# Differential attention: the next head's projections spread over eighteen of the twenty steps of a head's values, in place of sixteen

## The chip, the cores and the metric

The kernel runs on one core of one Trainium2 chip. The metric is the time on the device in microseconds (us) of one launch. Everything is fp32; matrix products are made of fp32r halves (a rounded `hi` and the rest `lo`), three matmuls for each product.

## What is computed

Two transformer blocks on a sequence of 1024 rows of width 1024. The first (pooling, gated linear attention, forgetting attention, a gated MLP) is not touched. The second is differential attention with 8 heads, each of two query and key parts of 64 and a value of 128, over 256 context keys and 1024 own keys:

```python
q, k, v, z = jnp.split(h @ w_in, 4, axis=-1)      # q and k of the own rows are rotated (axial rope)
s = jnp.einsum('bqhzd,bkhzd->bhzqk', q, k)
p = jax.nn.softmax(s, axis=-1)
a = p[:, :, 0] - lam * p[:, :, 1]
o = jnp.einsum('bhqk,bkhe->bqhe', a, v)
o = o * lax.rsqrt(jnp.mean(o * o, axis=-1, keepdims=True) + SUBLN_EPS) * subln_gain * (1 - lambda_init)
y = (o * jax.nn.silu(z)) @ w_out
```

An output projection, a residual and a last norm follow.

## The kernel before

`differential_attention` (L2099) runs on the five engines, each with its own program; semaphores alone order them. The engines call `heads` (L2183): scores of head 0, then for each head `values` (its attention times V) and the scores of the next head. Heads 0 to 6 run `values(h, True)`, which also projects Q and K of head h + 1; head 7 runs `values(7, False)` without that.

**Pieces and units.** The projections of a head are pieces: `TILE` (L2106) gives pieces 0 and 1 as the two halves of Q, 2 and 3 as the halves of K, 4 as K of the context, 5 and 6 as z; V has three more. Each piece takes 8 units (`contract`, L2705: k = 0 to 7), each unit three matmuls of 512 columns, or 256 for the context. Pieces 0 to 4 belong to `values`, the rest to `scores`. A piece's PSUM bank is `BANK` (L2108): banks 1, 2, 1, 2, 1.

**The spread.** `spread` (L2115) deals the 40 units of pieces 0 to 4, a context unit counting half, into `SHARING + 1` slots. The first slot is `before`, which TensorE runs ahead of the steps; the others are `chunks[n]`, run in step n. With SHARING = 16 these are the units (piece and k):

```
before: 00 01 02
chunks: 0: 03 04   1: 05 06   2: 07 10   3: 11 12   4: 13 14   5: 15 16   6: 17 20   7: 21 22 23   8: 24 25
        9: 26 27  10: 30 31  11: 32 33  12: 34 35  13: 36 37  14: 40 41 42 43  15: 44 45 46 47   16 to 19: none
end = [2, 6, 9, 13, 15]
```

`end[p]` (L2127) is the step in which piece p is finished. The lists `next_head` of ScalarE (L2391) and VectorE (L2597) place their work on piece p by it, and these engines work strictly in the order of their program.

**A step on TensorE** (`values`, L2801, 20 steps: 10 key tiles for each half g of the queries): `turn(n + 2)` (L2758) makes four 128x128 transposes of the probabilities into one of three banks; `times_v(n)` (L2774) makes three matmuls with V, and waits for `lo(n)` of VectorE; then the units of `chunks[n]`. In step 0 the product comes behind the units. Step 12 ends with `squares(h, 0)` (L2785), the sum of squares of the first half's output; steps 16 and 17 and the end of the loop have `turn_v` 0, 1 and 2 (L2737), transposes of the next head's V. `turn_v(1)` waits until the shuffle of piece 3 has read bank 2. `score(h + 1, 0, 0)` (L2745), the first work of the next stage, waits for all splits of Q and K (`qk_done`) and for two of the three splits of V (`v_done`).

**ScalarE in step n** (L2435): `hi(n + 2)` (L2411) rounds the transposed probabilities out of PSUM; then `next_head(n)`: `qk_hi` (L2324) of piece p at `end[p] + 2` and `+ 3` (the two parts z), of piece 4 at `end[3] + 3`; the rounding of the k weights at 2 and of the z weights at 8; `v_hi` (L2344) of V at 16, 18 and 19, the last behind `output` and `square` of the previous half; then `silu_z` at 3 and 5, `output` (L2354) at 10, `square` (L2359) at 11, `rstd` (L2363) at 13, each with what it waits for.

**VectorE in step n** (L2624): `lo(n + 2)` (L2583); then `next_head(n)`: `terms` (L2532: the cosine product and the shuffle) of piece p at `end[p]`, `rotated` (L2540: the add of cosine and sine terms) at `end[p] + 1`, `qk_lo` (L2545) at `+ 2` and `+ 3`, of piece 4 at `end[3] + 3`; `v_lo` (L2555) at 16, 18 and 19; and `gated` (L2588) at 14. Where several fall in one step, pieces come in order, and V last.

**GpSimd** (L2288): the rest `lo` of the k weights (`subtract_lo`, L2078), the sine terms (L2275) of pieces 0, 1 and 2, the rest of the z weights, the sine term of piece 3, then the rest of the v weights of the head after (`next_v`). **SyncE** (L2227): the second rope half once the terms of piece 0 are made, the z weights once piece 1 is done (`done(h + 1, 1)`), the first rope half after the terms of piece 2, then the store of the first half of the output.

Of the kernel before, what the change touches and what calls it, by code (L numbers as in the profile page):

```python
# [2098 lines left out]
def differential_attention(core, ph, mix_at, lead):  # L2099
# [15 lines left out]
    def spread(units, slots):  # L2115

        share, spent, out = sum(u[2] for u in units) / slots, 0.0, [[] for _ in range(slots)]
        for p, k, c in units:
            out[min(int(spent / share), slots - 1)].append((p, k))
            spent += c  # L2120
        return out


    SHARING = 16
    before, *chunks = spread([(p, k, 0.5 if FROM[p] == CONTEXT else 1.0) for p in range(5) for k in range(KT)], SHARING + 1)
    chunks += [[] for _ in range(STEPS - SHARING)]
    end = [max(n for n in range(STEPS) if (p, KT - 1) in chunks[n]) for p in range(5)]  # L2127
# [826 lines left out]
def program(nc, d):  # L2954

    with ExitStack() as ctx:
        core = Core(nc, ctx, d)
        with ExitStack() as first:
            mix_at = next_place(nc)
            mix = first.enter_context(nc.sbuf_tensor("mix", [P, KT, SEQ], F32))  # L2960
            with ExitStack() as rows:
                gate_rows = rows.enter_context(nc.sbuf_tensor("gate_rows", [P, SEQ], F32))
                mixers(core, mix, mix_at, gate_rows)
            core.clear_semaphores()
            hid_at = next_place(nc)
            hid = first.enter_context(nc.sbuf_tensor("hid", [P, FT, SEQ], F32))
            with Phase(core, "wo") as po, Phase(core, "gu") as pg, Phase(core, "down") as pd, Phase(core, "diff") as ph:
                lead = second_half(core, po, pg, pd, mix, mix_at, hid, hid_at)
                differential_attention(core, ph, mix_at, lead)
            core.clear_semaphores()  # L2970
        with ExitStack() as last:
            feat = last.enter_context(nc.sbuf_tensor("feat", [P, KT, SEQ], F32))
            block_output(core, feat)
# [97 lines left out]
```

How the kernel before makes its waits and increments, by code:

```python
    def __call__(self, ins):  # L66
        self.n += 1
        ins.then_inc(self.sem, 1)
        self.eng.wait_ge(self.sem, self.base + self.n)
# [90 lines left out]
    def load(self, sync, i, c, src):  # L160
        b = self.bufs[c]
        if self.in_place:
            self.wait_free(sync, i, c)
        elif self.raw.shape[1] == 2:
            sync.wait_ge(self.lo[b], self.nth(i, c) + 1)
        elif c:
            sync.wait_ge(self.lo[self.bufs[c - 1]], self.nth(i, c - 1) + 2)
        else:
            final = len(self.bufs) - 1
            before = self.bufs[final]
            sync.wait_ge(self.lo[before], self.nth(i, final) + 2 - self.uses[before])
        sync.dma_start(self.raw[:, self.raw_of[b], :], src).then_inc(self.loaded[b], 16)
# [1 line left out]
    def wait_free(self, eng, i, c):  # L175
        b = self.bufs[c]
        before = [x for x in range(c) if self.bufs[x] == b]
        if before:
            eng.wait_ge(self.piece_done, (i + 1) * self.pieces + self.last[before[-1]] + 1)
        else:
            final = [x for x in range(len(self.bufs)) if self.bufs[x] == b][-1]
            eng.wait_ge(self.piece_done, i * self.pieces + self.last[final] + 1)
# [1 line left out]
    def round_hi(self, act, i, c):  # L185
        b = self.bufs[c]
        act.wait_ge(self.loaded[b], self.nth(i, c) * 16 + 16)
        if not self.in_place:
            self.wait_free(act, i, c)
        act.activation(self.core.wh[:, b, :], self.raw[:, self.raw_of[b], :], ACT.Copy).then_inc(self.hi[b], 1)
```

## Time and profile before

| | us |
|---|---|
| median of 3 runs | 2386.15 |
| lowest and highest | 2385.19, 2386.16 |
| the profiled execution's own time | 2389.79 |
| its span | 2387.9 |
| TensorE busy | 2177.1 (91%) |
| VectorE, ScalarE, GpSimd busy | 1240.7, 993.4, 619.3 |

The span is the time from the first to the last instruction of the profiled execution; its own time lies 1.9 us above it. In the rows further down, times are us from the start of the span; a row of the timeline gives start, duration, engine, line, operation, what it writes and reads, and in brackets the engine's idle time before it with the instruction that ended it. The differential attention's stages of values and scores run from about 1482 to 2262.

### The profile page before, as it was taken

The page shows a single profiled execution, that of the slowest core. Times are in us where ns is not written, and L with a number is a line of the kernel's source. Part 1 is how long each engine was busy: PE and PEld are TensorE (multiplying, and loading weights), DVE is VectorE, ACT ScalarE, POOL GpSimd, SP SyncE. Part 2 cuts the span into 40 slices and gives each one's busy share as a digit, 9 for nine tenths or more (in the row PEclk, how much of TensorE's full clock was granted, in tenths as well). Part 3 has the DMA queues.
Part 4 walks back from the last instruction along what each step waited for, and adds up shares of the span by engine and source line. Part 5 has one row for each costly group of instructions (what it writes and reads, how often), then busy time and mean ns, then how long its engine had stood idle before and what let it go on. Part 6 is the DMA issues. An engine that isn't in the chain of part 4 may idle for free. (4 is left out here: it accounts for less than half of the span.)

```text
span 2387.9 us, 28748 instructions
## 1 busy us (share of the span) xinstructions
PE 2177.1 (91%) x10344; PEld 1772.4 (74%) x10344; DVE 1240.7 (52%) x1650; ACT 993.4 (42%) x1546; POOL 619.3 (26%) x387
## 2 busy tenths in 40 slices
PE   6998888888999999789999987999999999998668
PEld 5886777766888888678887866877778777786557
DVE  4645534435322212132445455877768777677553
ACT  4434434434311111121224344565656656566531
POOL 2212122254022222122344532212222222221140
PEclk9999999989999999899999988999999999999989
DMA  3100000004222221121423421111010110100052
GB/s 110 49 28 26 27 9 26 18 1 159 97 88 79 70 79 61 53 106 61 150 97 117 138 97 71 35 37 36 28 46 32 42 35 26 48 31 27 9 194 106
DMA packets 46687, 152.38 MB, mean 64 GB/s; under 512 B 6160, under 2 KB 6576, under 8 KB 46496
## 3 DMA queue, kind: packets, MB, share of 16 engines
q1 hardware_dynamic: 42768, 137.68, 16.8%
q0 software_dynamic: 3856, 13.86, 1.7%
q8 instruction: 39, 0.64, 0.1%
q14 instruction: 24, 0.20, 0.0%
HBM read 132.38 MB, written 18.88 MB: 63 GB/s over the span
## 5 line engine op out<-in xcount | busy, mean ns | idle before, releaser
L214 PE MATMUL psum<-h_hi,w_hi 128*128 128x512 f32 x704 | 276.2, 392 | 22.5 <-POOL w_lo L199 22.5
L215 PE MATMUL psum<-h_lo,w_hi 128*128 128x512 f32 x704 | 275.6, 391 | 0.0
L216 PE MATMUL psum<-h_hi,w_lo 128*128 128x512 f32 x704 | 275.4, 391 | 0.0
L2378 ACT ACTIVATE diff_probs<-psum,diff_neg_max 128x1280 f32<-128x1280 f32 x128 | 170.3, 1330 | 130.1 <-DVE diff_neg_max L2563 129.3
L2563 DVE TENSOR_REDUCE diff_neg_max<-psum 128x1 f32<-128x1280 f32 x128 | 189.5, 1487 | 56.1 <-PE psum L2035 56.0
L199 POOL TENSOR_TENSOR w_lo<-w_whole,w_hi 128x1024 fp32r<-128x1024 f32 x44 | 107.2, 2439 | 391.4 <-ACT w_hi L190 391.4
L2092 PE MATMUL psum<-h_hi,w_hi 128*128 128x512 f32 x496 | 200.8, 405 | 6.5 <-DVE h_lo L1463 3.9
L1823 DVE SCALAR_TENSOR_TENSOR gu_ada_product<-gu_ada_w,gu_cond 128x1024 f32<-128x1024 f32 x48 | 91.1, 1898 | 214.3 <-DMA gu_ada_w<-in_ada_w 211.3
L2093 PE MATMUL psum<-h_lo,w_hi 128*128 128x512 f32 x496 | 196.4, 396 | 0.0
L2094 PE MATMUL psum<-h_hi,w_lo 128*128 128x512 f32 x496 | 195.9, 395 | 0.0
L214 PEld LDWEIGHTS psum<-h_hi,w_hi 128*128 128x128 f32 x704 | 133.2, 189 | 51.5 <-issue 23.6
L1834 DVE TENSOR_TENSOR down_a_lo<-hid,down_a_hi 128x512 fp32r<-128x512 f32 x44 | 101.6, 2310 | 128.6 <-ACT down_a_hi L1743 126.4
L2034 PE MATMUL psum<-diff_k_hi_lo,diff_q_hi_twice 128*128 128x512 f32 (+1 forms) x384 | 142.5, 371 | 24.7 <-DVE diff_v_lo L2558 13.4
L2283 POOL TENSOR_SCALAR diff_probs<-diff_probs,diff_recip 128x1280 f32<-128x1280 f32 x64 | 85.9, 1342 | 291.7 <-DVE diff_probs L2580 291.7
L390 PE MATMUL psum<-h_hi,w_hi 128*128 128x512 f32 x368 | 153.6, 417 | 2.5 <-POOL w_lo L379 1.4
L216 PEld LDWEIGHTS psum<-h_hi,w_lo 128*128 128x128 f32 x704 | 133.1, 189 | 28.0
L215 PEld LDWEIGHTS psum<-h_lo,w_hi 128*128 128x128 f32 x704 | 133.3, 189 | 27.4
L391 PE MATMUL psum<-h_lo,w_hi 128*128 128x512 f32 x368 | 146.9, 399 | 0.0
L392 PE MATMUL psum<-h_hi,w_lo 128*128 128x512 f32 x368 | 146.8, 399 | 0.0
L190 ACT ACTIVATE w_hi<-w_whole 128x1024 fp32r<-128x1024 f32 x44 | 46.5, 1061 | 238.3 <-DMA w_whole<-in_w_gu 238.2
L1657 POOL TENSOR_TENSOR w_lo<-down_w_raw,w_hi 128x1024 fp32r<-128x1024 f32 x42 | 101.0, 2407 | 135.7 <-ACT w_hi L1741 135.7
L2035 PE MATMUL psum<-diff_k_hi_lo,diff_q_lo_twice 128*128 128x512 f32 (+1 forms) x384 | 132.0, 359 | 0.0
(374 smaller groups left out, 4883.7 us busy)
## 6 DMA issues: line engine op xcount, KB each, us to landing
w_whole<-in_w_gu SPq DMA_DIRECT2D x44, 512.0 KB, 3.4
down_w_raw<-in_w_down SPq DMA_DIRECT2D x44, 512.0 KB, 3.4
w_whole<-in_da_w_in SPq DMA_DIRECT2D x31, 512.0 KB, 3.5
gu_ada_w<-in_ada_w SPq DMA_DIRECT2D x24, 512.0 KB, 4.3
w_whole<-in_w_in SPq DMA_DIRECT2D x23, 512.0 KB, 3.4
diff_rope_half<-in_rope SPq DMA_DIRECT2D x17, 512.0 KB, 4.1
mix<-in_x SPq DMA_DIRECT2D x8, 512.0 KB, 8.7
wo_w_raw<-in_w_o SPq DMA_DIRECT2D x8, 512.0 KB, 3.4
```

What stands on the lines that cost most here:

```text
L214: pe.matmul(out, wh, rh, start=(k == 0), stop=False)
L215: pe.matmul(out, wh, rl, start=False, stop=False)
L216: last = pe.matmul(out, wl, rh, start=False, stop=(k == KT - 1))
L390: pe.matmul(out, wh, rh, start=(k == 0), stop=False)
L391: pe.matmul(out, wh, rl, start=False, stop=False)
L392: last = pe.matmul(out, wl, rh, start=False, stop=(k == KT - 1))
L2034: pe.matmul(out, self.q_hi[:, z, queries], self.k[:, z, keys], start=True, stop=False)
L2092: pe.matmul(out, wh, rh, start=(k == 0), stop=False)
L2093: pe.matmul(out, wh, rl, start=False, stop=False)
L2094: last = pe.matmul(out, wl, rh, start=False, stop=(k == KT - 1))
L2378: act.activation(dst, core.psum[:, 1536 * z:1536 * z + NKEY], ACT.Exp, bias=nm[:, qb % 2, z:z + 1], accum_out=rs[:, qb % 2, z:z + 1]).then ...
L2563: dve.tensor_reduce(nm[:, qb % 2, z:z + 1], core.psum[:, 1536 * z:1536 * z + NKEY], AX.X, ALU.max, negate=True).then_inc(s[f"max{z}"], 1)
```

## The change

```diff
-    SHARING = 16
+    SHARING = 18
     before, *chunks = spread([(p, k, 0.5 if FROM[p] == CONTEXT else 1.0) for p in range(5) for k in range(KT)], SHARING + 1)
     chunks += [[] for _ in range(STEPS - SHARING)]
     end = [max(n for n in range(STEPS) if (p, KT - 1) in chunks[n]) for p in range(5)]
```

The lists become:

```
before: 00 01
chunks: 0: 02 03   1: 04 05   2: 06 07   3: 10 11   4: 12 13   5: 14 15   6: 16 17   7: 20 21   8: 22   9: 23 24
       10: 25 26  11: 27 30  12: 31 32  13: 33 34  14: 35 36  15: 37 40  16: 41 42 43 44  17: 45 46 47  18, 19: none
end = [2, 6, 11, 15, 17]
```

Nothing else is changed: the same instructions are issued, in another order on TensorE, ScalarE and VectorE.

## Rows read from the trace of the kernel before

**Rows 1.** The page: busy time of TensorE, and issue to landing of a weight load.
```profile
PE 2177.1 (91%) x10344; PEld 1772.4 (74%) x10344; DVE 1240.7 (52%) x1650; ACT 993.4 (42%) x1546; POOL 619.3 (26%) x387
...
w_whole<-in_da_w_in SPq DMA_DIRECT2D x31, 512.0 KB, 3.5
```

**Rows 2.** Waits of TensorE, 1484 to 2185 us: total, times, longest.
```profile
PE psum L2780 <- DVE diff_pt_lo L2585: 14.8, 14, 1.9
PE psum L2787 <- ACT diff_rstd L2361: 6.7, 7, 1.0
```

**Rows 3.** Timeline of TensorE: the first product with V of heads 0, 1, 2.
```profile
1534.08 0.50 PE L2780 MATMUL psum<-diff_pt_hi,diff_v_hi 128*128 128x512 f32 x1 [0.56 <-DVE diff_pt_lo L2585]
...
1634.97 0.50 PE L2780 MATMUL psum<-diff_pt_hi,diff_v_hi 128*128 128x512 f32 x1 [0.21 <-DVE diff_pt_lo L2585]
...
1734.37 0.50 PE L2780 MATMUL psum<-diff_pt_hi,diff_v_hi 128*128 128x512 f32 x1 [0.20 <-DVE diff_pt_lo L2585]
```

**Rows 4.** Stretches behind heads 0 and 1: busy PE, PEld, DVE, ACT, POOL; PEclk, DMA.
```profile
1582.20:1585.60 3.40, 3.40 (x12) 2.51 (x10) 1.32 (x2) 2.42 (x4) 0.77 (x1) 0.52 0.00 0
1683.10:1686.50 3.40, 3.40 (x17) 2.50 (x16) 1.82 (x2) 2.44 (x5) 0.75 (x1) 1.00 0.00 0
```

**Rows 5.** Timeline of TensorE, head 0: step 10 and the start of step 11's product.
```profile
1558.54 0.48 PE L2780 MATMUL psum<-diff_pt_hi,diff_v_hi 128*128 128x512 f32 x1
...
1559.32 0.39 PE L2092 MATMUL psum<-h_hi,w_hi 128*128 128x512 f32 x1
...
1560.01 0.39 PE L2092 MATMUL psum<-h_hi,w_hi 128*128 128x512 f32 x1
...
1561.05 0.48 PE L2780 MATMUL psum<-diff_pt_third,diff_v_hi 128*128 128x512 f32 x1
```

**Rows 6.** Timeline of TensorE, head 0: `squares` of step 12, two context units of step 14.
```profile
1566.85 1.12 PE L2787 MATMUL psum<-diff_rstd,diff_ones 128*128 128x512 f32 x2 [0.97 <-ACT diff_rstd L2361]
1567.81 0.60 PE L2770 MATMUL psum<-ident,diff_probs 128*128 128x128 f32 x4
...
1571.46 0.28 PE L2092 MATMUL psum<-hc_hi,w_hi 128*128 128x256 f32 x1
...
1571.81 0.28 PE L2092 MATMUL psum<-hc_hi,w_hi 128*128 128x256 f32 x1
```

**Rows 7.** Timeline of TensorE, head 0: the last product and the next head's first score.
```profile
1581.31 0.50 PE L2780 MATMUL psum<-diff_pt_hi,diff_v_hi 128*128 128x512 f32 x1 [1.87 <-DVE diff_pt_lo L2585]
...
1582.24 0.72 PE L2034 MATMUL psum<-diff_k_hi_lo,diff_q_hi_twice 128*128 128x512 f32 x1
```

**Rows 8.** Timelines of VectorE and GpSimd, head 0: piece 2 (K, second half).
```profile
1560.02 0.69 DVE L2537 TENSOR_TENSOR diff_rope_cos<-psum,diff_rope_half 128x512 f32<-128x512 f32 x1
...
1562.85 2.80 DVE L2543 TENSOR_TENSOR diff_rope_cos<-diff_rope_cos,diff_rope_sin 128x512 f32<-128x512 f32 x1 [0.92 <-POOL diff_rope_sin L2277]
...
1562.70 2.40 POOL L2081 TENSOR_TENSOR w_lo<-w_whole,w_hi 128x1024 fp32r<-128x1024 f32 x1
```

**Rows 9.** Timeline of ScalarE, head 0: `rstd` begins, and `hi(16)` behind it.
```profile
1569.14 1.28 ACT L2365 ACT_TABLE_LOAD   x1
...
1572.98 0.58 ACT L2416 ACTIVATE diff_pt_hi<-psum 128x512 fp32r<-128x512 f32 x1
```

**Rows 10.** Timeline of VectorE, head 0: from `lo(16)` to `v_lo(1)`, 12 rows in all.
```profile
1573.59 0.69 DVE L2585 TENSOR_TENSOR diff_pt_lo<-psum,diff_pt_hi 128x512 fp32r<-128x512 f32 x1 [1.70 <-ACT diff_pt_hi L2416]
1574.20 0.68 DVE L2543 TENSOR_TENSOR diff_rope_cos<-diff_rope_cos,diff_rope_sin 128x512 f32<-128x512 f32 x1
1574.80 0.75 DVE L2592 SCALAR_TENSOR_TENSOR diff_rstd<-diff_o,subg,diff_rstd 128x512 f32<-128x512 f32 x1
...
1576.19 0.68 DVE L2585 TENSOR_TENSOR diff_pt_third<-psum,diff_pt_third 128x512 fp32r<-128x512 f32 x1
...
1579.06 0.88 DVE L2030 TENSOR_TENSOR diff_k_hi_lo<-psum,diff_k_hi_lo 64x256 fp32r<-64x256 f32 x2
...
1581.17 0.68 DVE L2558 TENSOR_TENSOR diff_v_lo<-psum,diff_v_hi 128x512 fp32r<-128x512 f32 x1
```

## The prediction

> **What bounds the kernel now.** The page comes first: TensorE is busy for 91% of the span [rows 1]. The change touches only `values(h, True)`, the value stage of seven of the eight heads, so I then read the waits of TensorE over those heads. Two are large: the products with V wait for VectorE's `lo` (L2585), 14.8 us in 14 waits, two in each head, and `squares` waits for ScalarE (L2361), 6.7 us in seven [rows 2]. The rest of the time it streams. The spacing of the heads is the yardstick: from the first product with V of one head (call it zero) to that of the next is 100.89 us after head 0 and 99.40 after head 1 [rows 3]. The 1.5 us between them is the clock: right behind zero + 48 head 0 runs at 0.52 of full clock, the 1.2 GHz level, where head 1 runs at 1.00 [rows 4]. Of the seven boundaries two (after heads 0 and 4) show that; it follows an idle TensorE.
>
> **Prices on TensorE** (start to start). The three products of a step take 0.78 us (1558.54 to 1559.32), a full unit, three matmuls of `contract`, takes 0.69, and the whole step with two units 2.51 (1558.54 to 1561.05), so that its `turn` has 0.35; with one unit it is 1.82, with none 1.13 [rows 5]. The step-12 `squares` takes 0.96, and ahead of it TensorE is idle 0.97, or 1.13 with the drain of its pipeline (a matmul lasts 0.39 but the next may start after 0.23). A context unit takes 0.35 (1571.46 to 1571.81) [rows 6].
>
> **The tail of a head now.** The last product starts 47.23 us after zero, after an idle of 1.87, or 2.03 with the drain. The first score of the next head starts at zero + 48.16 [rows 3, 7]. Of these 48.16 us, 1.13 + 2.03 = 3.16 are waits and 45.0 are work.
>
> **What the change does to the lists.** With 19 slots in place of 17, `before` falls from three units to two, steps 7 and 8 from three and two to two and one, and the units lost there move behind; the last full unit ends in step 15 in place of 13, the context units lie in 15 to 17 in place of 14 and 15. `end` goes from [2, 6, 9, 13, 15] to [2, 6, 11, 15, 17]. No instruction is added or taken away. But `end` also sets where ScalarE and VectorE handle the pieces: `terms`, `rotated` and the splits of piece 2 and of piece 3 move two steps later.
>
> **First term, a loss: the unit that leaves `before`.** It lies ahead of zero, where TensorE already waits for `lo(0)`: 0.56 us in head 0, 0.21 in head 1, 0.20 in head 2 [rows 3]. `lo(0)` hangs on the last maximum, exponential and combination of the scores, none of which waits for `before`. So zero does not come earlier; 0.69 us of work moves from ahead of it to behind it. Work behind zero: 45.0 + 0.69 = 45.69.
>
> **Second term, a gain: step 12.** Today `square` on ScalarE stands behind `qk_hi` of piece 2 (both at n = 11), and that waits for `rotated`. This add takes 2.80 us, where the same add of piece 3 takes 0.68 [rows 10]; it starts 0.15 us after GpSimd began the 2.40 us subtraction of the z weights, queued right behind the sine term [rows 8]. With `end[2]` at 11, `qk_hi` comes at n = 13 and `square` runs at once. The 1.13 us goes.
>
> A rule says what the collision is. The Trainium skill (SBUF — State Buffer, "Who interferes with whom") holds that VectorE with two SBUF inputs and a GpSimd instruction that reads SBUF exclude each other, the later one blocked until the first is done. The row agrees: the subtraction ends at 1565.10, and 0.68 later is 1565.78, seen 1565.65 [rows 8, 10]. By the rule the add would cost its plain 0.68 if it ever came first.
>
> **Third term: the tail, hand-timed from zero.** Step 11's product starts 26.97 after zero today and, two units fewer behind it, at 25.60. Piece 2 is out at +1.64 (0.78, 0.69 and 0.17 of drain): 27.2. `rotated` starts 2.83 after `terms` [rows 8]: 30.1. GpSimd's order is unchanged, so the z subtraction again runs just ahead of it and it ends at 32.9. Now ScalarE: `qk_hi(2,0)` at n = 13 ends at 33.6, and only then comes `rstd`, queued behind it, 3.9 us long with its two table loads; `hi(16)` starts 3.84 after the first load [rows 9], at 37.4, and `lo(16)` at 38.0. TensorE wants `lo(16)` at 38.8 and loses nothing yet. But VectorE is backlogged: `lo(16)`, `qk_lo(2,1)`, the two of `gated`, `lo(17)`. At the spacings of today's tail (0.6 for an operation with nothing to wait for, 0.72 for a 64-row split, 1.4 for `gated`; twelve groups stand from 1573.59 to 1581.17 [rows 10]) `terms` of piece 3 starts at 41.5, though the piece is out at 38.2. Its chain is serial: `rotated` at 41.5 + 2.83 = 44.3, then `v_lo(0)` and `lo(19)` 0.6 apart, ending at 46.2. The last product, which TensorE could start at 44.75, starts at 46.3: a wait of 1.5 in place of 2.03, a gain of 0.5. Behind `lo(19)` stand both splits of piece 3 (0.72 each, their `qk_hi` could not start before 45.0), the context pair (0.9) and `v_lo(1)` (0.7): over at 49.3. The first score waits for all of these (`qk_done` and `v_done`; it overwrites banks 1 and 2, which they read), and TensorE, ready at 46.3 + 0.93 = 47.2, starts it at **49.4**: a new wait of 2.2. Today these splits are over at 1581.85 = zero + 47.8 and cost nothing there, because they run while step 19 waits.
>
> **Sum of a head:** +0.69 - 1.13 - 0.50 + 2.16 = **+1.2 us**, or 49.4 against 48.16. Seven heads: +8.5 us. By the rule, with the add first, `rotated` ends at 30.8, ScalarE's `hi(15)` (until 32.5) bounds instead, and all behind comes 0.4 earlier: +0.8 a head, +5.6 in all.
>
> **Costed at nothing.** Piece 1 ends one unit (0.69) later, hence the z load issues at zero + 16.2 and lands 3.5 us later [rows 1] at 19.7; ScalarE reaches that rounding near 21.0. The cover is 1.3 us. SyncE's `first_rope` waits for the sine term of piece 2 (30.0 in place of 28.7), and the rope half is wanted at 41.5. The store behind it waits for `gated` anyway. GpSimd's last sine term comes later, with only the v weights behind it. `turn_v(1)` waits for the shuffle of piece 3 (42.9) and TensorE is there at 43.6; if VectorE were 0.7 later, this would cost too.
>
> **Fourth term, the clock.** No row prices it for the new pattern, an idle of 1.4, a busy microsecond, an idle of 2. Bounds: no boundary slow, -3.0 us against today's two; all seven slow, +7.5. The nearest row is today's single idle of 1.87, which led to the low level in two of seven; the new pattern is idler. I take four of seven, +3.0.
>
> **Total:** +11.5 us on the median of 2386.15 gives 2397.7. The profiled execution took 2389.79, 3.6 above the median; its terms are differences and carry over.
>
> **The rivals.**
> *TensorE-bound to the end (faster).* The filled steps 16 and 17 hide VectorE's tail, so that TensorE never waits behind zero: 48.16 - 45.69 = 2.47 saved a head, 17.3 in all, 2368.9. For it: TensorE alone could do it, and the work is the same. Against: it needs `v_lo(1)` over by 45.6, while piece 3 alone, out at 38.2, with the chain above takes until 46. Any gain over 0.2% needs the score at 47.5 or earlier. Chance 0.10 for this and what lies between.
> *No change.* VectorE packs the tail at 0.60 throughout and the z collision misses: 0.4 and 0.6 less, +0.2 a head, with the clock as today 2387.5. Chance 0.14.
> *The clock falls in all seven* in place of four: 8.5 + 7.5, 2402.2. The more idle boundary speaks for it, the five undisturbed boundaries after 1.87 us of idle against it. Chance 0.20.
> *The forecast,* 2390.9 to 2400: chance 0.56. That the change does nothing is no case: the lists are built by arithmetic and differ.
>
> **Numbers.** About 0.2%, 4.8 us, is what a measurement of this kernel can tell. Slower 0.56 + 0.20 = 0.76, same 0.14, faster 0.10. The range 2385 to 2406 takes in most of the no-change case below, and above all seven clock falls with 0.5 us a head more on the chain (+3.5).
>
> **What would show it.** Right: `squares` at step 12 without a wait; seven waits of the scores L2034 for `v_lo` L2558 of about 2 us; the last product's wait down to 1.4; zero to zero 100.6 us at full clock; `rotated` at 2.80 seven times. Wrong: the first score before zero + 48.2, a wait inside steps 13 to 17, or a wait at zero that did not grow by 0.7.

## The result and the profile after

The change makes the kernel slower: 2402.99 us (median of 6, 2399.38 to 2407.90) against 2386.15 (6 runs, 2385.15 to 2387.66), ratio 1.0072 with a 95% interval of 1.0059 to 1.0085. The forecast was 2397.7, between 2385 and 2406. The profiled execution took 2401.97, its span is 2400.1 us; against the profiled execution of before that is 12.2 us more, and the reading below accounts for these 12.2.

The waits of TensorE over the same seven heads (us in total, times, longest), for [rows 2]:

```profile
PE psum L2780 <- DVE diff_pt_lo L2585: 13.9, 14, 1.3
PE psum L2034 <- DVE diff_v_lo L2558: 13.3, 7, 2.0
```

The wait of `squares` (L2787) is gone, seven times 0.97. In its place the first score of the next head (L2034) waits seven times 1.9 us for `v_lo`. The 14 waits of the products changed inside: 0.68 at zero, 1.30 at the last product, where they were 0.2 (0.56 in head 0) and 1.87.

The timeline of TensorE, kernel after: first products of heads 0 to 2, and in head 0 `squares`, the last product and the next head's first score, for [rows 3, 6, 7]:

```profile
1534.12 0.50 PE L2780 MATMUL psum<-diff_pt_hi,diff_v_hi 128*128 128x512 f32 x1 [0.68 <-DVE diff_pt_lo L2585]
...
1634.65 0.50 PE L2780 MATMUL psum<-diff_pt_hi,diff_v_hi 128*128 128x512 f32 x1 [0.68 <-DVE diff_pt_lo L2585]
...
1736.81 0.50 PE L2780 MATMUL psum<-diff_pt_hi,diff_v_hi 128*128 128x512 f32 x1 [0.68 <-DVE diff_pt_lo L2585]
...
1564.42 1.02 PE L2787 MATMUL psum<-diff_rstd,diff_ones 128*128 128x512 f32 x2
...
1580.36 0.50 PE L2780 MATMUL psum<-diff_pt_hi,diff_v_hi 128*128 128x512 f32 x1 [1.30 <-DVE diff_pt_lo L2585]
...
1583.43 0.50 PE L2034 MATMUL psum<-diff_k_hi_lo,diff_q_hi_twice 128*128 128x512 f32 x1 [1.89 <-DVE diff_v_lo L2558]
```

Count from the first product, 1534.12: the last product starts at 46.24 (47.23 before), a microsecond earlier, and yet the first score comes at 49.31 (48.16 before). The next head's zero lies 100.53 later where the clock stays up and 102.16 where it falls, against 99.40 and 100.89.

VectorE in the tail of head 0, kernel after, for [rows 8, 10]:

```profile
1561.42 0.69 DVE L2537 TENSOR_TENSOR diff_rope_cos<-psum,diff_rope_half 128x512 f32<-128x512 f32 x1
...
1564.24 2.78 DVE L2543 TENSOR_TENSOR diff_rope_cos<-diff_rope_cos,diff_rope_sin 128x512 f32<-128x512 f32 x1 [0.30 <-POOL diff_rope_sin L2277]
...
1572.15 0.69 DVE L2585 TENSOR_TENSOR diff_pt_lo<-psum,diff_pt_hi 128x512 fp32r<-128x512 f32 x1 [3.74 <-ACT diff_pt_hi L2416]
1572.87 0.69 DVE L2030 TENSOR_TENSOR diff_k_hi_lo<-diff_rope_cos,diff_k_hi_lo 64x512 fp32r<-64x512 f32 x1
1573.59 0.76 DVE L2592 SCALAR_TENSOR_TENSOR diff_rstd<-diff_o,subg,diff_rstd 128x512 f32<-128x512 f32 x1
1574.38 0.69 DVE L2595 TENSOR_TENSOR diff_rstd<-diff_rstd,diff_silu_z 128x512 f32<-128x512 f32 x1
1574.99 0.68 DVE L2585 TENSOR_TENSOR diff_pt_third<-psum,diff_pt_third 128x512 fp32r<-128x512 f32 x1
1575.59 0.68 DVE L2537 TENSOR_TENSOR diff_rope_cos<-psum,diff_rope_half 128x512 f32<-128x512 f32 x1
...
1578.42 0.69 DVE L2543 TENSOR_TENSOR diff_rope_cos<-diff_rope_cos,diff_rope_sin 128x512 f32<-128x512 f32 x1 [0.91 <-POOL diff_rope_sin L2277]
...
1582.68 1.02 DVE L2558 TENSOR_TENSOR diff_v_lo<-psum,diff_v_hi 128x512 fp32r<-128x512 f32 x2
```

Read it downwards: `lo(16)` waits for ScalarE until zero + 38.0; five operations stand ahead of the cosine term of piece 3 (L2537), which starts at 41.5; its `rotated` (L2543) follows 2.83 later; the last row, two of the `v_lo`, runs past the first score's start at 49.3. ScalarE's `rstd` is what made `lo(16)` late, behind `qk_hi` of piece 2 (for [rows 9]):

```profile
1567.05 0.63 ACT L2026 ACTIVATE diff_k_hi_lo<-diff_rope_cos 64x512 fp32r<-64x512 f32 x1 [0.46 <-DVE diff_rope_cos L2543]
1567.70 1.28 ACT L2365 ACT_TABLE_LOAD   x1
...
1571.54 0.58 ACT L2416 ACTIVATE diff_pt_hi<-psum 128x512 fp32r<-128x512 f32 x1
```

The clock behind the boundaries (PEclk is the third number from the right), for [rows 4]: behind head 0 full, behind heads 1 to 5 low, behind head 6 full. Two of the seven rows:

```profile
1583.40:1586.80 3.40, 3.37 (x14) 2.50 (x15) 1.80 (x2) 1.17 (x2) 2.38 (x1) 1.00 0.00 0
1684.30:1687.30 3.00, 3.00 (x9) 2.08 (x8) 0.95 (x1) 0.41 (x1) 2.36 (x1) 0.50 0.00 0
```

So the difference is about 7 x 1.15 = 8.0 for the later first score and 3 x 1.55 = 4.7 for five low-clock boundaries in place of two. Measured directly, from the zero of head 0 to the zero of head 7 the profiled execution takes 710.0 us (1534.12 to 2244.11) where it took 697.1 (1534.08 to 2231.16), 12.9 more; the rest of the span took 0.7 less, which makes the 12.2.

### The profile page after: what moved, and what is told of

Read it like the earlier page. It is cut to its first block and busy times, and to the rows that moved or that the text cites. A ratio compares the mean times of both kernels' runs of the same rounds, so it can differ in the third digit from the quotient of the medians.

```text
span 2400.1 us, 28748 instructions
## 1 busy us (share of the span) xinstructions
PE 2183.0 (91%) x10344; PEld 1775.8 (74%) x10344; DVE 1237.9 (52%) x1650; ACT 993.1 (41%) x1546; POOL 618.1 (26%) x387
## 5 line engine op out<-in xcount | busy, mean ns | idle before, releaser
L2034 PE MATMUL psum<-diff_k_hi_lo,diff_q_hi_twice 128*128 128x512 f32 (+1 forms) x384 | 142.8, 372 | 38.1 <-DVE diff_v_lo L2558 26.8
```

The source lines that it names most:

```text
L2034: pe.matmul(out, self.q_hi[:, z, queries], self.k[:, z, keys], start=True, stop=False)
```

## The experiments

Each is compared with the kernel before, run on the same chip in the same session. Its median there was 2386.2 to 2390.6, and the four sessions of the experiments were on four different chips, so the ratios are to be compared, not the times. "First score" and "zero" are as in the prediction; unless a range is given a figure held within 0.05 us in heads 0 to 5.

| kernel | first score at zero + | low clock, of 7 | ratio (95%) | zero 0 to zero 7, us |
|---|---|---|---|---|
| the kernel before | 48.17 | 2 | 1 | 697.1 |
| changed (18) | 49.3 | 5 | 1.0072 (1.0059 to 1.0085) | 710.0 |
| both idle stretches filled | 49.3 | 0 | 1.0019 (1.0010 to 1.0028) | 702.5 |
| only the first filled | 49.3 | 5 | 1.0064 (1.0049 to 1.0080) | 711.2 |
| only the second filled | 49.3 | 0 | 1.0015 (1.0006 to 1.0024) | 702.7 |
| `gated` a step later | 49.3 | 6 | 1.0064 (1.0050 to 1.0078) | 713.6 |
| `gated` on 16 columns | 48.27 | 3 | 1.0016 (1.0006 to 1.0026) | 700.7 |
| z rest ahead of the sine term | 48.86 | 4 | 1.0039 (1.0025 to 1.0053) | 707.7 |
| three units in `before` | 49.3 | 6 | 1.0063 (1.0050 to 1.0077) | 713.7 |
| five units ahead of zero | 48.60 | 7 | 1.0052 (1.0038 to 1.0065) | 716.7 |
| the same, both idles filled | 48.60 | 0 | 1.0013 (1.0003 to 1.0023) | 697.1 |
| SHARING = 17 | 48.84 | 3 | 1.0035 (1.0021 to 1.0048) | 704.4 |
| before, z rest early | 46.94 | 3 | 0.9965 (0.9953 to 0.9977) | 691.1 |
| the same, idle filled | 46.94 | 0 | 0.9954 (0.9941 to 0.9968) | 686.6 |

The columns of low clock and of the time from the zero of head 0 to the zero of head 7 are of the profiled execution only. Outside these two zeros the runs change next to nothing, and yet that part of the span took between 1686.6 and 1693.8 us in the 14 profiled executions. So a single time carries up to seven microseconds that have nothing to do with the change, and the last column, though of one execution, leaves that part out. In "before, z rest early" the first score comes at 47.3 to 47.4 in two heads, in which the clock is low already ahead of it.

### The clock: filling TensorE's idle time

```diff
+                def fill(count):
+                    for _ in range(count):
+                        pe.matmul(ps[5][:, :], core.wh[:, 0, 0:P], turned_hi(18), start=True, stop=True)
...
+                        if n == 19 and more:
+                            fill(5)
                         if n:
                             times_v(h, n)
...
                     if more:
                         turn_v(h + 1, 2)
+                        fill(8)
```

> The changed kernel, and in the two idle stretches of TensorE at the end of a head it multiplies 5 and 8 extra times (512 columns, 0.23 us each, so 1.2 of the 1.3 us and 1.8 of the 2.0 us idle) into bank 5, whose result nobody reads. No wait is taken away. Clock theory (the idle pair at the end of a head lets TensorE's clock fall to the lower level right behind it, 1.5 us a time): the low level disappears at all seven boundaries, zero to zero is 100.6 everywhere (first score still at zero + 49.3), and the time falls to the sum of the tail alone, 2386 + 7 x 1.15 = 2394 (8 to 10 us under the changed kernel). Rival (the clock falls for other reasons, or the rest of the 16.8 us is elsewhere): the heads of 102.1 stay and the time stays at 2400 to 2405.

The first score stayed where it was (zero to zero 100.46 to 100.54 in heads 0 to 5) and the low level disappeared at all seven boundaries. Two of the seven rows, kernel with both stretches filled:

```profile
1684.00:1687.00 3.00, 2.97 (x13) 2.17 (x13) 1.80 (x2) 0.80 (x1) 2.12 (x1) 1.00 0.00 0
1784.50:1787.50 3.00, 2.96 (x13) 2.17 (x13) 1.81 (x2) 0.82 (x1) 2.10 (x1) 1.00 0.00 0
```

The ratio fell from 1.0072 to 1.0019, 12.7 us in 2390, where 8 to 10 were expected; between the zeros the profiled executions differ by 7.5 (710.0 to 702.5), and only these are shown to be the clock. The expectation of 2394 forgot that the kernel before pays for low clock too; the ratio, +4.5 us, fits 8.0 less those 3. More work on TensorE made the kernel faster: an idle stretch costs its own length and, where the clock falls behind it, the low clock too.

> The changed kernel with the five extra multiplies ahead of the last product alone; the wait of 1.9 ahead of the first score is left open. Clock theory in its pair form (it takes both idle stretches): no low level behind the boundaries, as with both filled, about 2393. Rival (the wait ahead of the score does it alone, as the single 1.87 of the kernel before did in two of seven): low level behind two to five of the seven.

> The changed kernel with the eight extra multiplies ahead of the first score alone; the wait of 1.3 ahead of the last product is left open. Pair form: no low level at the boundaries, about 2393. Rival (any idle of over a microsecond at this place may do it): some of the seven still show it.

The pair form fell. With only the 1.3 us ahead of the last product filled, five of the seven boundaries were low, as unchanged; with only the wait of the first score filled, none. It is the idle of 1.9 ahead of the first score that brings the low level; the 1.3 us alone did not in seven cases. A stretch behind head 1 in each, first filled and second filled:

```profile
1682.00:1685.00 3.00, 3.00 (x9) 2.02 (x9) 1.43 (x2) 0.74 (x1) 2.18 (x1) 0.63 0.00 0
```

```profile
1680.60:1683.60 3.00, 2.98 (x13) 2.19 (x13) 1.79 (x2) 0.79 (x1) 2.13 (x1) 1.00 0.00 0
```

Why an idle of the same length (1.87 before, 1.89 after) gave two of seven in the one kernel and five of seven in the other stays open. The length alone does not decide it: in the run with `gated` a step later (below) the wait of the first score was 1.87 to 1.89 in heads 0 to 5, and the clock stayed up behind head 1 but fell behind heads 0 and 2 to 6.

### The backlog on VectorE

```diff
-                        if n == 14:
+                        if n == (15 if more else 14):
                             gated(h, 0)
```

> The changed kernel with VectorE's two operations of gated(h, 0) in step 15 in place of step 14, so behind the cosine and shuffle of piece 3 and not ahead of them. Same work, same count. Backlog theory (piece 3 is out at zero + 38.2 and VectorE reaches it only at 41.5 because lo(16), a split and gated stand ahead): terms of piece 3 starts 1.4 earlier at 40.1, gated fills the 0.9 idle before rotated, the first score comes at about zero + 48.3 in place of 49.3, -1.0 us a head, -7 us in all (2396), and fewer low-clock stretches may add up to 7 more. Rival (the tail is bound by the arrival of the piece itself, so by TensorE's place for the units): the first score stays at 49.3 and the time within 1 us.

The first score did not move. But the timeline shows that this is not the rival's reason. Kernel with `gated` a step later, VectorE and GpSimd in head 1 (zero is 1638.47):

```profile
1678.54 0.68 DVE L2537 TENSOR_TENSOR diff_rope_cos<-psum,diff_rope_half 128x512 f32<-128x512 f32 x1
...
1679.79 0.73 DVE L2592 SCALAR_TENSOR_TENSOR diff_rstd<-diff_o,subg,diff_rstd 128x512 f32<-128x512 f32 x1
1680.55 1.67 DVE L2595 TENSOR_TENSOR diff_rstd<-diff_rstd,diff_silu_z 128x512 f32<-128x512 f32 x1
1682.15 0.68 DVE L2585 TENSOR_TENSOR diff_pt_lo<-psum,diff_pt_hi 128x512 fp32r<-128x512 f32 x1
1682.75 0.68 DVE L2543 TENSOR_TENSOR diff_rope_cos<-diff_rope_cos,diff_rope_sin 128x512 f32<-128x512 f32 x1
```

```profile
1679.97 1.70 POOL L2277 TENSOR_TENSOR diff_rope_sin<-diff_rope_sin,diff_rope_half 128x512 f32<-128x512 f32 x1 [9.16 <-DVE diff_rope_sin L2538]
```

`terms` of piece 3 did start 1.4 earlier (zero + 40.07), as the theory wanted. But `gated` then ran against the sine term of the same piece: both lengthened, 1.67 in place of 0.69 and 1.70 in place of 1.29, and `rotated` began at 44.28 as ever. The run moved the work from ahead of the chain into it. So the next one left the work's place and cut its size, the third argument being the columns of both operations:

```diff
-                            gated(h, 0)
+                            gated(h, 0, 16 if more else HALF)
```

> The changed kernel with the two operations of gated(h, 0) in heads 0 to 6 on 16 columns in place of 512 (the other columns of that half are left ungated): their place and waits stay, some 1.1 to 1.2 us of VectorE's work goes from between lo(16) and lo(17). It avoids what spoilt the run with gated one step later, where the first score stayed at zero + 49.3 because the second operation of gated then ran against GpSimd's sine term and took 1.67 in place of 0.69. Backlog theory: terms of piece 3 starts at 40.3 in place of 41.5 and everything serial behind it comes as much earlier, first score at 48.1 to 48.2, -8 us in seven heads, and perhaps less low clock. Rival (piece 3's own arrival or ScalarE sets the tail): first score within 0.2 of 49.3.

Kernel with `gated` on 16 columns, VectorE, then TensorE, head 2:

```profile
1778.35 0.23 DVE L2592 SCALAR_TENSOR_TENSOR diff_rstd<-diff_o,subg,diff_rstd 128x16 f32<-128x16 f32 x1
1778.62 0.18 DVE L2595 TENSOR_TENSOR diff_rstd<-diff_rstd,diff_silu_z 128x16 f32<-128x16 f32 x1
...
1779.32 0.68 DVE L2537 TENSOR_TENSOR diff_rope_cos<-psum,diff_rope_half 128x512 f32<-128x512 f32 x1
```

```profile
1738.89 0.50 PE L2780 MATMUL psum<-diff_pt_hi,diff_v_hi 128*128 128x512 f32 x1 [0.69 <-DVE diff_pt_lo L2585]
...
1787.16 0.50 PE L2034 MATMUL psum<-diff_k_hi_lo,diff_q_hi_twice 128*128 128x512 f32 x1 [1.89 <-DVE diff_v_lo L2558]
```

A microsecond taken from VectorE between `lo(16)` and `lo(17)` moved the cosine term of piece 3 to zero + 40.4 and the first score to 48.27, in every head. Piece 3 had been out since 38.2 in both. That shows the backlog in the chain. The ratio is 1.0016, or 13 us under the changed kernel: 7 of them are the chain, about 3 the two low boundaries fewer; the rest is not accounted for, and between the zeros of the profiled executions the difference is 9.3 (710.0 to 700.7).

```diff
-                        for j in range(3):
+                        for j in range(2):
                             sine_term(h + 1, j)
                         ws.subtract_lo(pool, h + 1, "z")
-                        sine_term(h + 1, 3)
+                        for j in range(2, 4):
+                            sine_term(h + 1, j)
```

> The changed kernel with GpSimd's subtraction for the z weights ahead of the sine term of piece 2 and not behind it; the z weights are rounded by zero + 22, the sine term starts at 28.7, so it no longer falls on rotated of piece 2. Theory: rotated drops from 2.78 to 0.69 in seven heads, rstd starts when hi(15) and qk_hi(2,0) allow, 0.4 earlier, and the first score comes at zero + 48.9: -0.4 a head, -3 us in all (2400). Rival (the collision sets the whole tail): -2.1 a head, the first score at 47.2, -15 us.

Kernel changed, z rest early: `rotated` of piece 2 in head 1 (zero is 1632.54), then ScalarE's `hi(15)`, the split behind it and the table load of `rstd`:

```profile
1662.66 0.69 DVE L2544 TENSOR_TENSOR diff_rope_cos<-diff_rope_cos,diff_rope_sin 128x512 f32<-128x512 f32 x1 [0.30 <-POOL diff_rope_sin L2277]
```

```profile
1664.41 0.60 ACT L2417 ACTIVATE diff_pt_hi<-psum 128x512 fp32r<-128x512 f32 x1 [2.78 <-PE psum L2771]
1665.04 0.63 ACT L2026 ACTIVATE diff_k_hi_lo<-diff_rope_cos 64x512 fp32r<-64x512 f32 x1
1665.68 1.28 ACT L2366 ACT_TABLE_LOAD   x1
```

All 28 `rotated` of heads 0 to 6 took 0.69, and the first score came at 48.86: 0.44 earlier, the predicted 0.4. The collision was a small part of the changed kernel's tail, since without it the split waits for `hi(15)`: `rstd` begins at zero + 33.14 in place of 33.58.

### The unit ahead of zero

> The changed kernel with the first unit of step 0 run in before again: three units ahead of zero, one in step 0, everything else of the changed lists. First-term theory: TensorE has idle time ahead of zero that this unit fills for nothing, so all behind zero comes 0.69 earlier (step 12's product at 27.4, last product 45.6, first score 48.6), -4.8 us in seven heads. Rival (the tail on VectorE and ScalarE is bound by something that does not move with TensorE, or zero moves 0.7 later): first score stays at 49.3 or zero to zero stays 100.5.

This run tested nothing, by a fault of its design: moving a unit from step 0 into `before` leaves four units ahead of zero, because step 0's units precede the first product. Nothing behind zero moved. Its repair takes one unit from step 1 as well:

```diff
+    before, chunks[0], chunks[1] = before + chunks[0][:1], chunks[0][1:] + chunks[1][:1], chunks[1][1:]
     chunks += [[] for _ in range(STEPS - SHARING)]
```

> The run with three units in before left four units ahead of zero, as the changed kernel has, since the units of step 0 also lie ahead of the first product; it could not test the first term. Here three units are in before, two in step 0 and one in step 1: five ahead of zero, as in the kernel before; the lists from step 2 on are the changed ones. First-term theory: TensorE's wait at zero falls to about 0.2, zero itself stays, step 12's product comes at 27.45 in place of 28.14 and the first score at 48.6 in place of 49.3: -0.69 a head, -4.8 us. Rival: first score stays at 49.3, or zero moves by as much.

The chain moved as the first term says: step 12's product at 27.45, first score at 48.60, 0.70 earlier, wait at zero 0.16 to 0.22 in heads 1 to 6. The time did not follow, ratio 1.0052. In the profiled execution (2411.25, the slowest of its five) all seven boundaries were low, and for longer, zero to zero 102.5:

```profile
1685.50:1691.50 6.00, 6.00 (x14) 4.16 (x15) 1.71 (x2) 2.12 (x3) 2.36 (x1) 0.52 0.00 0
```

Six microseconds at half clock, where the changed kernel shows about three. Three other runs show the long form once, behind head 0 (zero to zero 103.24 with `gated` a step later, 102.91 with the z rest early, 103.25 with three units in `before`). To take the clock out, the same lists with both idle stretches filled:

> Five units ahead of zero put the first score at 48.6 but its heads also ran longer at the low clock (102.5 from zero to zero), so its time says nothing of the first term. Here the same lists with the extra multiplies in both idle stretches (5 and 8), as in the first run. First-term theory: first score at 48.6, zero to zero 99.8 in place of 100.5, no low level at the seven boundaries, and 4.8 us under that first run, so a ratio of 1.000 to the kernel before in place of 1.0019. Rival: zero to zero 100.5 and the time of the first run.

TensorE, head 1: first product, first score, next first product:

```profile
1629.79 0.50 PE L2781 MATMUL psum<-diff_pt_hi,diff_v_hi 128*128 128x512 f32 x1 [0.16 <-DVE diff_pt_lo L2586]
...
1678.39 0.50 PE L2034 MATMUL psum<-diff_k_hi_lo,diff_q_hi_twice 128*128 128x512 f32 x1
...
1729.61 0.49 PE L2781 MATMUL psum<-diff_pt_hi,diff_v_hi 128*128 128x512 f32 x1 [0.17 <-DVE diff_pt_lo L2586]
```

Zero to zero is 99.8, 0.7 under the run without the moved unit, in heads 0 to 5, and the clock is full at all seven boundaries. From zero 0 to zero 7 it takes 697.1, 5.4 under that run and as long as in the kernel before, which has two low boundaries. In time the step is smaller than expected: the ratio is 1.0013 (1.0003 to 1.0023) against 1.0019 (1.0010 to 1.0028), 1.4 us in place of 4.8, with intervals that allow either. The first term is shown in the trace and is not resolved in the time.

### Half the change, and the version that beats both

> SHARING = 17, halfway: before has two units, piece 2 ends in step 10, piece 3 in step 14, the context in 16. Backlog theory, by the same hand timing: square is free at step 12 (-1.13), qk_hi of piece 2 is ahead of rstd only with its second part; lo(16) at zero + 38.3, terms of piece 3 at 38.9 directly behind it, gated after it; last product 45.6, first score 47.9 against 48.16 before and 49.3 at 18: about -0.3 us a head against the kernel before, with fewer idle pairs: 2381 to 2386. Rival (dose: each added step costs in proportion): halfway between, about 48.7, 2394.

It missed: 48.84 and ratio 1.0035, which on 2386.15 is 2394.5. These are the numbers of the rival, 48.7 and 2394. VectorE in head 1 (zero is 1630.83):

```profile
1670.93 0.73 DVE L2592 SCALAR_TENSOR_TENSOR diff_rstd<-diff_o,subg,diff_rstd 128x512 f32<-128x512 f32 x1
1671.70 1.67 DVE L2595 TENSOR_TENSOR diff_rstd<-diff_rstd,diff_silu_z 128x512 f32<-128x512 f32 x1
```

The hand timing held until `gated`: `terms` of piece 3 starts at 38.87, where 38.9 was expected, and `gated` at 40.10. Here too it meets the sine term of piece 3, and its second operation takes 1.67 in place of 0.69, about the 0.9 by which the first score was late. It is the miss of the run with `gated` a step later. No run takes the collision out at SHARING = 17, so that the lost 0.9 is due to it alone is argued, not shown.

> The kernel before with the subtraction for the z weights ahead of the sine term of piece 2. Theory: rotated of piece 2 takes 0.69 in place of 2.80, so qk_hi and square on ScalarE run at once, step 12's wait of 1.13 goes, and the tail, which hangs on TensorE's step 13 by way of rstd, comes 1.1 earlier as a whole: first score at 47.0, zero to zero 98.3, -7.9 us: ratio 0.9967 to the kernel before. Rival (the wait only moves, into the last product): first score stays at 48.2, ratio 1.000.

Kernel before with the z rest early: `rotated` of piece 2 in head 1, then the last product and the first score:

```profile
1657.93 0.69 DVE L2544 TENSOR_TENSOR diff_rope_cos<-diff_rope_cos,diff_rope_sin 128x512 f32<-128x512 f32 x1 [0.91 <-POOL diff_rope_sin L2277]
```

```profile
1674.54 0.50 PE L2781 MATMUL psum<-diff_pt_hi,diff_v_hi 128*128 128x512 f32 x1 [1.87 <-DVE diff_pt_lo L2586]
...
1675.47 0.48 PE L2034 MATMUL psum<-diff_k_hi_lo,diff_q_hi_twice 128*128 128x512 f32 x1
```

Zero is 1628.55, so the first score comes at 46.92. `squares` no longer waits, and the whole tail is 1.2 us earlier: ratio 0.9965, expected 0.9967. So the gain that the change made at step 12 was to be had by one swap on GpSimd, without the new tail. The swap is worth 1.2 us a head in the kernel before and 0.44 in the changed one, because only in the first does TensorE itself wait behind the collision.

> The same, and seven extra multiplies (512 columns, 0.23 us each, 1.6 of the 2.0 us) into bank 5 in the idle stretch ahead of the last product; their result is not read. Clock theory: no low level behind any of the seven boundaries, some 0 to 3 us less than without them. Rival: no difference, or slower by up to 1.6 us a head if the idle stretch is no longer there.

Ratio 0.9954 (0.9941 to 0.9968), median 2378.95 against 2389.80: the fastest of the runs here, and no low clock at the seven boundaries. The step from the run without the extra multiplies, about 2.5 us, is in the expected 0 to 3; the two intervals overlap, so it is not settled by the times. The low clock went from three boundaries to none, and the time between the zeros from 691.1 to 686.6.

## Why the prediction was right

**First term, the unit that leaves `before`** (+0.69): right as a cost behind zero, 0.70 in two runs that put it back. The sign that was named for it was mis-sized: the wait at zero grew by 0.5, from 0.2 to 0.68, in heads 1 to 5, not by 0.7, and in head 0 by 0.12 alone. The rest is lost a little earlier, in the twelve transposes of `turn` 0 to 2 ahead of zero. They take 1.41 us in place of 1.23 in head 2; in head 0 `turn(2)` waits 0.35 for the last exponential, which TensorE now reaches earlier.

**Second term, step 12** (-1.13): right; the wait is gone in all seven heads, and `rotated` still takes 2.78, the collision being where it was.

**Third term, the tail**: right to 0.1 us, and no wait of TensorE appeared in steps 13 to 17, as what was costed at nothing had it. `lo(16)` at 38.0, `terms` of piece 3 at 41.5, `rotated` at 44.3, last product at 46.24 (46.3), first score at 49.31 (49.4). The two runs on `gated` and the early z rest show its two sources, the backlog (1.0 us when cut by a microsecond) and the late `rstd` (0.4). What the prediction did not see is how narrow the place is: one step later and `gated` collides with the sine term.

**Fourth term, the clock**: the direction was right, the size short. It took four low boundaries at 1.5 us, the profile has five at 1.6, so 4.7 to 5 us more than before in place of 3.0. Four was a choice between bounds and not worked out, so that it came close is partly luck. How many fell in the other executions is not known. The pattern was also named wrongly: the prediction priced a pair of idles, and the wait of the first score brings the low level alone.

**The rivals.** *TensorE-bound to the end* needed the last split over by 45.6; it is over past 49. *No change* needed the collision to be missed; it came seven times. The measured 2402.99 lies above the forecast's own band of 2390.9 to 2400 and nearest to the third rival, the clock falling everywhere, at 2402.2. The profile does not bear that rival out: two of its seven boundaries kept the full clock.

**The sum**: 8.5 + 3.0 = 11.5 forecast; 12.9 between the zeros and 12.2 in the span of the profiled pair; 16.8 in the medians. The profiled execution of before lay 3.6 above its median, that of after 1.0 below, which is the 4.6 between the last two. What makes it up is not traced: the profile has one execution of each kernel, the part outside the zeros spreads by 7 us, and the median of before came out at 2389.6 to 2390.6 in three later sessions and at 2386.8 in a fourth.

## What to carry to other kernels

Spreading filler work over more steps also moves the point at which each piece is finished, and with it everything that other engines do to it; price that serial chain from the piece's end to its last consumer, with what is queued ahead of it, before counting the idle slots to be filled. Where an operation is four times as long as its twin, look at what GpSimd does at that moment: here reordering two of its instructions made the kernel 0.35% faster, while the change made it 0.72% slower. And a TensorE wait of about 2 us can cost nearly as much again behind it in clock (1.6 us a boundary in the changed kernel), so in a kernel of this kind idle stretches are to be judged with the granted clock beside them.

## What was not expected of the hardware

- Extra multiplies whose results nobody reads made the changed kernel faster, by 7.5 us between the zeros and 12.7 by the ratios. They kept TensorE at 2.4 GHz (granted clock 1.00) behind all seven boundaries. Placed only in the idle stretch of 1.3 us they left five of them low, placed only in that of 1.9 none.
- An idle stretch of the same length (1.9 us) led to no low clock, to about 3 us, or to 6 us of it, the last in all seven heads of one execution and behind head 0 of three others.
- GpSimd is lengthened too: its sine term took 1.70 in place of 1.29 when `gated` ran beside it. The first operation of `gated` (1679.79 to 1680.52) had started 0.18 ahead of the sine term, and the second ended 0.55 after it: the rows fit each waiting for the other's instruction in turn. The Trainium skill (SBUF — State Buffer, "Who interferes with whom") says that whoever starts first holds the shared ports for its whole instruction and the other is blocked; these rows agree.
